# A two-layer streaming-encoder trunk: SSM powers without their zero halves on GpSimd, ScalarE spreading them out, modulation products and norms moved to other places

## The chip, the cores and the metric

One core of a Trainium2 chip runs the whole program in one launch. The time is device microseconds (us), the median of several executions. TensorE (PE) multiplies, VectorE (DVE) and ScalarE (ACT) work elementwise, GpSimd (POOL) too, SyncE (SP) issues DMAs; all five run their own instruction streams and wait for each other by semaphores.

## The reference

`x` is 256 tokens by 1024 channels, float32, batch 1. A conditioning vector `c` gives, for each of the two layers, six rows of 1024 values (shifts, scales, gates) by a 1024 x 6144 product.

```
for layer i:
    mod = silu(c) @ mod_w[i] + mod_b[i];  sh1, sc1, g1, sh2, sc2, g2 = split(mod, 6)
    h = rms_norm(x, g) * (1 + sc1) + sh1
    y = sparse_attention(h)            # layer 0: indexer scores, 64 kept keys per query, ALiBi, softmax
    y = s5_layer(h)                    # layer 1: diagonal complex state space model, gelu, GLU
    x = x + g1 * y
    h = rms_norm(x, g) * (1 + sc2) + sh2
    x = x + g2 * conv_ffn(h)           # up 1024 -> 5632, causal conv of width 3, silu gate, down 2816 -> 1024
return rms_norm(x, final_g)
```

The S5 layer has 64 groups of 16 channels with 64 complex states each: `h[t] = a * h[t-1] + Bbar u[t]`, `y[t] = Re(C h[t]) + d u[t]`. It is computed in chunks of 4 steps, for which the powers `a^k Bbar` and `C a^k`, k = 0 to 4, are needed.

## The kernel before, in words

All weights stream through one ring of six buffers `raw` (128 x 1024 floats, 512 KB each), loaded by SP in the order of use. Each weight tile is split into a rounded high part `whi` by ScalarE (`split_hi`, L749) and a low part `wlo` by VectorE (`split_lo`, L1039), three slots each. TensorE multiplies every tile three times, high by high, high by low and low by high (`three`, L345 to L347), 24 matmuls for one tile of 8 k-blocks. `slot_used`, `hi_ready`, `lo_ready` count tiles. The order on each engine is written out by hand.

The modulation product is cut into 24 pieces `c` (2 MB each), `gemv(c)` (L381): 16 matmuls of 2 columns into the PSUM bank `gv`. After each second piece ScalarE copies `gv` to `gm` (`row_out`), TensorE turns it into columns (`columns`, L392, with a 2-column matrix `picks`), and VectorE adds the bias (`col_out`, L1044). Pieces 0 to 5 stand in the projection phase, 6 to 13 in attention, and 14 to 23 (`C_FFN` = 14) in the first FFN, two for every four steps of its loop.

Phases in order of time: the first norm; six projection tiles in halves (`half(n, 0)`, then pieces 2 and 3 and `columns(1)`, then `half(n, 1)`); the indexer scores with pieces 4 and 5; 24 more projection tiles with the top-k rounds of VectorE; attention over 8 head pairs; the output projection (8 tiles); `norm(1)`; the FFN of layer 0 (22 steps of two up tiles and one down tile each, `up_step` and `down_step`); `norm(2)`; the S5 input projection interleaved with the state space work; the GLU (16 tiles); `norm(3)`; the FFN of layer 1, the same loop with no modulation pieces; the last norm. A norm takes squares on ScalarE (L768), sums them on TensorE into `gv` (L426), makes a column of them (L433), takes the root, and spreads it (L443); then VectorE and ScalarE make `hh` and `hl` for the next product, block by block (`norm_out`, L1063 and L1068; `norm_hi`, L785).

GpSimd makes the powers while the first FFN runs: `times` is one complex product, six instructions of 128 x 1024 (L1545 to L1555). Two groups of 16 channels stand side by side on partitions 0 to 63 and 64 to 127, and in the layout `p (pair, 32 channels)` the half that belongs to the other group is zero; these zeros are loaded and multiplied. There are 43 such instructions before `pw` = `PW_K`; `pace` lets two go for each step of the FFN (it waits on `a_lo`). The last power, six more, comes after `k_done` in `norm(2)`. TensorE uses the powers in `lag_kernels` (L632), which waits for `pw`.

## Time and profile before

| | us |
|---|---|
| median of 3 executions | 802.56 (801.44 to 803.48) |
| the profiled execution | 801.77 |
| its span, first to last instruction | 800.0 |
| PE busy | 742.9 (93%) |
| DVE busy | 584.6 (73%) |
| ACT busy | 389.0 (49%) |
| POOL busy | 175.4 (22%) |

The profile is of one execution. "Busy" excludes waits; the granted clock is a share of TensorE's full speed. A share over the whole span is an average over phases with different limits, so the phases are read one by one.

### The profile page before, as it was taken

Reading aid. Unit: us, or ns where it says so; the run is one execution under the profiler, and the core shown is the slowest. Engines: PE = TensorE matmul, PEld = TensorE weight load, DVE = VectorE, ACT = ScalarE, POOL = GpSimd, SP = SyncE. Lnnn points to the kernel's source line nnn. Section 1 sums busy time; section 2 is a strip of 40 time slices with the busy share of each in tenths; the row PEclk is TensorE's granted clock in tenths of the full one; section 3 lists DMA queues with packets and bytes.
Section 4 is the critical chain, followed back from the end, with each engine's and each line's share of the span. In section 5 each row is a group of like instructions: output and inputs, shape, how many; then the busy total and the mean of one; then the engine's idle time right before and its main releaser. Section 6 shows DMA issues by size and latency. Waiting matters only on the chain.

```text
span 800.0 us, 17708 instructions
## 1 busy us (share of the span) xinstructions
PE 742.9 (93%) x6676; PEld 675.5 (84%) x6676; DVE 584.6 (73%) x948; ACT 389.0 (49%) x656; POOL 175.4 (22%) x115
## 2 busy tenths in 40 slices
PE   5778999999899999999999798989989999999996
PEld 1667999559798889898989688988979999999994
DVE  5666555984778888888998875686657667666675
ACT  4255445555464445444445442324456555555554
POOL 0000000301336444544444515542000000000000
PEclk9889999999899999999999889999999999999998
DMA  9898554896346776767775211112634555555531
GB/s 330 340 350 343 194 182 135 327 401 251 127 168 241 258 258 247 270 242 255 246 259 171 93 53 55 54 56 78 195 124 146 196 174 193 174 178 194 168 100 53
DMA packets 46842, 157.51 MB, mean 197 GB/s; under 512 B 6352, under 2 KB 7888, under 8 KB 46800
## 3 DMA queue, kind: packets, MB, share of 16 engines
q1 hardware_dynamic: 44064, 148.46, 53.3%
q10 hardware_dynamic: 2160, 6.38, 2.0%
q0 software_dynamic: 576, 2.10, 0.7%
q8 instruction: 28, 0.46, 0.2%
q14 instruction: 14, 0.11, 0.0%
HBM read 155.87 MB, written 1.05 MB: 196 GB/s over the span
## 4 chain that ended last, share of the span: by engine, by line
PE 62%; DVE 18%; issue 9%; ACT 6%; DMA 2%; SPq 1%; POOL 1%; DVEq 1%; ACTq 0%; POOLq 0%
PE up L345 10%; PE up L347 10%; PE up L346 10%; DVE wlo L1039 8%; PE acc L345 7%; PE acc L346 6%; PE acc L347 6%; ACT whi L749 3%; DVE ffn L1341 3%; PE gv L381 3%; DVE hl L1068 1%; DMA ffn<-in_mw 1%; DMA arena<-in_mw 1%; PE up L697 1%; PE acc L672 1%
## 5 line engine op out<-in xcount | busy, mean ns | idle before, releaser
L1039 DVE TENSOR_TENSOR wlo<-raw,whi 128x1024 fp32r<-128x1024 f32 x188 | 297.2, 1597 | 93.9 <-ACT whi L749 86.6
L345 PE MATMUL up<-hh,whi 128*128 128x256 f32 x896 | 257.3, 287 | 1.3 <-DVE hl L1068 0.8
L346 PE MATMUL up<-hl,whi 128*128 128x256 f32 x896 | 255.3, 285 | 0.0
L347 PE MATMUL up<-hh,wlo 128*128 128x256 f32 x896 | 255.2, 285 | 0.0
L749 ACT ACTIVATE whi<-raw 128x1024 fp32r<-128x1024 f32 x185 | 191.7, 1051 | 35.7 <-PE acc L347 24.4
L345 PEld LDWEIGHTS up<-hh,whi 128*128 128x128 f32 x896 | 173.8, 194 | 11.5 <-issue 9.9
L346 PEld LDWEIGHTS up<-hl,whi 128*128 128x128 f32 x896 | 173.9, 194 | 0.0
L347 PEld LDWEIGHTS up<-hh,wlo 128*128 128x128 f32 x896 | 173.7, 194 | 0.0
L345 PE MATMUL acc<-ah,whi 128*128 128x256 f32 x352 | 100.4, 285 | 6.8 <-DVE wlo L1039 6.6
L346 PE MATMUL acc<-al,whi 128*128 128x256 f32 x352 | 99.6, 283 | 0.0
L347 PE MATMUL acc<-ah,wlo 128*128 128x256 f32 x352 | 99.5, 283 | 0.0
L1341 DVE SCALAR_TENSOR_TENSOR ffn<-up,conv,ffn 128x254 f32<-128x254 f32 (+1 forms) x176 | 72.5, 472 | 32.3 <-ACT ffn L914 32.3
L345 PE MATMUL acc<-hh,whi 128*128 128x256 f32 x256 | 77.5, 303 | 9.6 <-DVE hl L1068 6.0
L914 ACT ACTIVATE ffn<-up,conv 128x256 f32<-128x256 f32 x88 | 44.9, 560 | 67.4 <-PE up L347 67.3
L346 PE MATMUL acc<-hl,whi 128*128 128x256 f32 x256 | 74.9, 292 | 0.0
L347 PE MATMUL acc<-hh,wlo 128*128 128x256 f32 x256 | 74.7, 292 | 0.0
L345 PEld LDWEIGHTS acc<-ah,whi 128*128 128x128 f32 x352 | 67.5, 192 | 8.4 <-DVE wlo L1039 8.4
L346 PEld LDWEIGHTS acc<-al,whi 128*128 128x128 f32 x352 | 67.5, 192 | 0.0
L347 PEld LDWEIGHTS acc<-ah,wlo 128*128 128x128 f32 x352 | 67.5, 192 | 0.0
L345 PEld LDWEIGHTS acc<-hh,whi 128*128 128x128 f32 x256 | 51.4, 201 | 13.8 <-issue 7.4
L346 PEld LDWEIGHTS acc<-hl,whi 128*128 128x128 f32 x256 | 51.7, 202 | 0.0
L347 PEld LDWEIGHTS acc<-hh,wlo 128*128 128x128 f32 x256 | 51.6, 202 | 0.0
(215 smaller groups left out, 963.1 us busy)
## 6 DMA issues: line engine op xcount, KB each, us to landing
raw<-in_w SPq DMA_DIRECT2D x188, 512.0 KB, 3.4
mraw<-in_mw SPq DMA_DIRECT2D x60, 512.0 KB, 6.2
arena<-in_mw SPq DMA_DIRECT2D x12, 512.0 KB, 11.6
raw<-in_w SPq DMA_DIRECT2D x12, 256.0 KB, 11.4
tmp<-in_mw SPq DMA_DIRECT2D x6, 512.0 KB, 7.7
ffn<-in_mw SPq DMA_DIRECT2D x6, 512.0 KB, 8.6
tmp<-in_mw ACTq DMA_DIRECT2D x4, 512.0 KB, 7.1
ffn<-in_mw ACTq DMA_DIRECT2D x4, 512.0 KB, 9.1
```

Of the source, the lines that this page charges most:

```text
L345: pe.matmul(out, w_h, xh, start=first, stop=False, skip_group_check=skip)
L346: pe.matmul(out, w_h, xl, start=False, stop=False, skip_group_check=skip)
L347: return pe.matmul(out, w_l, xh, start=False, stop=last, skip_group_check=skip)
L381: mm = pe.matmul(gv[32 * j:32 * j + 2, :], cond[:, k, 1 - odd:3 - odd], src[:, kk * 512:kk * 512 + 512], start=(k < 4 and not odd), stop=( ...
L672: mm = pe.matmul(acc[:, 2 + mt % 2, (2 * q + r) * NJ:(2 * q + r + 1) * NJ], bpow_r[:, r, c:c + P], ust[:, mt % 2, q, :], start=True, stop= ...
L697: mm = pe.matmul(y[32 * q:32 * q + 32, :, l], cpow[:, (l + 1) % 4, r, pair * 32:pair * 32 + 32], hst[:, r, q, :], start=False, stop=(l == ...
L749: act.activation(whi[:, n % SPL, :], raw[:, n % RAW, :], ACT.Copy).then_inc(hi_ready, 1)
L914: act.activation(cb[:, par, e, :], up[:, par, e * T:(e + 1) * T], ACT.Identity, scale=conv[:, layer, 2, ds(s + e * FT, 1)], bias=conv[:, l ...
L1039: dve.tensor_tensor(wlo[:, n % SPL, :], raw[:, n % RAW, :], whi[:, n % SPL, :].bitcast(F32), ALU.subtract).then_inc(lo_ready, 1)
L1068: dve.scalar_tensor_tensor(hl[:, k, :], tmp[:, k, :], modc[:, sh + k:sh + k + 1], hh[:, k, :].bitcast(F32), ALU.add, ALU.subtract).then_in ...
L1341: dve.scalar_tensor_tensor(cb[:, par, e, 1 + back:T], up[:, par, e * T:e * T + T - 1 - back], w, cb[:, par, e, 1 + back:T], ALU.mult, ALU. ...
```

## The change

- **Powers.** `b_re`, `b_im`, `c_re`, `c_im` are stored without the zero halves (256 KB each). `times` works on 128 x 512 in `turn_x`, `turn_b`, `turn_c`. After each finished power ScalarE writes it into the old layout: `pad`, two ACTIVATEs with a per-partition factor of 1 or 0 (`sides`), one for each half. In the first FFN a pad stands at the end of steps 5, 8, 11, 14, 15, 18 and 21, an eighth after `split_hi(W_SIN)` and before the squares of `norm(2)`, the ninth in the S5 loop. TensorE waits for `padded`.
- **Modulation pieces.** Piece 14 is multiplied inside `norm(1)` before the last square's sum, 15 after the spread, 16 to 20 in the first FFN, 21 in `norm(2)`, 22 and 23 in `norm(3)`. Pieces 15, 22 and 23 have their own places in `arena`; SP loads 22 and 23 after the S5 loop (`y_done`), ahead of the GLU tiles from the eighth on.
- **Columns.** From pair 2 on, `columns` is four 128 x 128 transposes, and VectorE sums the four partial rows (a reduce and an add in place of one add).
- **Norms.** The sums go to `misc`; the bank openings of the FFN stand in the waits of the norm.
- **First phases.** SP no longer loads the six small constants, GpSimd's queue does; `gemv(2)`, `gemv(3)` and `columns(1)` stand between the first halves; the indexer's scores and `gemv(5)` stand between projection tiles 6 to 11.

```diff
-C_PROJ, C_ATT, C_FFN = 4, 6, 14
+C_PROJ, C_ATT, C_OUT, C_FFN, C_SIN, C_GLU = 4, 6, 14, 16, 21, 22
-        t1, t2 = tpool[:, 0:1024], tpool[:, 1024:2048]
+        t1, t2 = tpool[:, 0:512], tpool[:, 512:1024]
+        turn_x = tpool[:, 1024:2048].rearrange(c_form, r=2, n=PR)
+        turn_b = cpow[:, 3, 0, :].rearrange(c_form, r=2, n=PR)
+        turn_c = cpow[:, 3, 1, :].rearrange(c_form, r=2, n=PR)
...
@@ SP
-            for dst, name in ((ones[:], "ones"), (epsc[:], "epsc"), (picks[:], "picks"), (ident[:], "ident")):
-                sp_.dma_start(dst, t[name]).then_inc(ones_in, 16)
             load_m(0)
-            for dst, name in ((modb[:], "modb"), (gains[:], "gains")):
-                sp_.dma_start(dst, t[name]).then_inc(early_in, 16)
...
+            for n in range(W_SIN, W_GLU + RAW + 1):
                 load_w(n)
-            first = W_SIN + 3
+            sp_.wait_ge(y_done, KT)
+            for c in range(2):
+                for s in range(MS):
+                    sp_.dma_start(last[:, MS * c + s, :], t["mw"][(C_GLU + c) * MS + s, :, :]).then_inc(m_late[1 + c], 16)
+            first = W_GLU + RAW + 1
@@ PE
-                    mm = pe.matmul(misc[:, 2 * q:2 * q + 2], gm[:, q * P:(q + 1) * P], picks[:], start=True, stop=True)
+                    if pair < 2:
+                        mm = pe.matmul(misc[:, 2 * q:2 * q + 2], gm[:, q * P:(q + 1) * P], picks[:], start=True, stop=True)
+                    else:
+                        mm = pe.transpose(misc[:, q * P:(q + 1) * P], gm[:, q * P:(q + 1) * P], ident[:])
...
                 for k in range(KT):
+                    if filler and k == KT - 1:
+                        filler()
                     pe.wait_ge(sq_ready, KT * n + k + 1)
...
-            for n in range(RAW):
-                half(n, 0)
+            half(0, 0)
             pe.wait_ge(gm_ready, 1)
             gemv(2)
+            half(1, 0)
+            half(2, 0)
             gemv(3)
+            half(3, 0)
             pe.wait_ge(hp_ready, 4)
             columns(1)
+            half(4, 0)
+            half(5, 0)
...
+            stream(6)
...
+            score(0, 1, T)
+            stream(7)
+            pe.wait_ge(idx_relu, 1)
+            score(1, 0, P)
+            stream(8)
+            gemv(C_PROJ + 1)
+            stream(9)
+            stream(10)
+            columns(C_PROJ // 2)
+            stream(11)
...
-            norm(1, C_FFN // 2, misc[:, T:2 * T])
+            norm(1, C_OUT // 2, misc[:, T:2 * T], open_rest, open_first, lambda: gemv(C_OUT))
+            gemv(C_OUT + 1)
...
-            for bank in (acc[:, 0, :], acc[:, 1, :], acc[:, 2, :], acc[:, 3, :], up[:, 0, :]):
-                open_bank(bank)
...
-                    with pe.Fori(0, 5) as i:
+                    two_steps(0, (C_OUT // 2, 0))
+                    with pe.Fori(0, 2) as i:
                         gemv(C_FFN, i)
-                        two_steps(2 * i)
+                        two_steps(4 * i + 1)
+                        two_steps(4 * i + 2)
                         gemv(C_FFN + 1, i)
-                        two_steps(2 * i + 1, i)
+                        two_steps(4 * i + 3, (C_FFN // 2, i))
+                        two_steps(4 * i + 4)
+                    gemv(C_SIN - 1)
+                    two_steps(9)
...
-            pe.wait_ge(pw, PW_K)
+            pe.wait_ge(padded, 2 * N_POW)
             lag_kernels(range(0, 5))
-            norm(2, CH, misc[:, T:2 * T], lambda: lag_kernels(range(5, KT - 1)))
+            norm(2, C_SIN // 2, misc[:, T:2 * T], lambda: lag_kernels(range(5, KT - 1)))
+            gemv(C_SIN)
...
                         project_two((acc[:, 0, 0:T], acc[:, 1, 0:T]), W_SIN, 3)
+                        columns(C_SIN // 2)
+                        pe.wait_ge(mod_col, C_GLU // 2)
...
-            norm(3, CH, misc[:, T:2 * T])
+            norm(3, C_GLU // 2, misc[:, T:2 * T], open_rest, open_first, lambda: gemv(C_GLU))
+            gemv(C_GLU + 1)
@@ ACT
+            def pad(src, dst, need):
+                act.wait_ge(pw, need)
+                for g in range(2):
+                    act.activation(dst.rearrange("p r n (g c) -> p r n g c", g=2)[:, :, :, g, :], src, ACT.Identity,
+                                   scale=sides[:, g:g + 1]).then_inc(padded, 1)
+            pads = {5: (turn_x, b_at(0), 6), 8: (turn_b, b_at(1), 12), 11: (turn_x, b_at(2), 18),
+                    14: (turn_b, b_at(3), 24), 15: (turn_c, c_at(0), 25), 18: (turn_x, c_at(1), 31),
+                    21: (turn_c, c_at(2), 37)}
...
+                    if layer == 0 and s in pads:
+                        pad(*pads[s])
...
             split_hi(W_SIN)
+            act.wait_ge(padded, 2 * (N_POW - 1))
+            pad(turn_x, c_at(3), PW_K)
             fetch_root()
...
+                    if m == 1:
+                        pad(raised, c_at(0), PW_ALL)
@@ DVE
+                if pair >= 2:
+                    parts = misc[:].rearrange("p (q j r) -> p r q j", q=4, j=4)[:, 0:2, :, :]
+                    dve.tensor_reduce(gsum[:].rearrange("p (e q) -> p e q", e=2), parts, AX.X, ALU.add).then_inc(part_sum, 1)
+                    dve.wait_ge(part_sum, pair + i - 1)
+                    dve.tensor_tensor(modc[:, ds(8 * (pair + i), 8)], gsum[:], modb[:, ds(8 * (pair + i), 8)],
+                                      ALU.add).then_inc(mod_col, 1)
+                    return
@@ POOL
+            for dst, name in ((ones[:], "ones"), (epsc[:], "epsc"), (picks[:], "picks"), (ident[:], "ident")):
+                pool.dma_start(dst, t[name]).then_inc(ones_in, 16)
...
-                return pr(name).unsqueeze(2).broadcast_to([P, PR, 32])
+                return pr(name).unsqueeze(2).broadcast_to([P, PR, 16])
...
-            pool.wait_ge(mod_used, 2 * CH * MS)
+            pool.wait_ge(mod_used, C_GLU * MS)
             pool.memset(mraw[:].rearrange("p a b -> p (a b)"), 0.0).then_inc(kz, 1)
...
-PW_FREE, PW_STEP = 3, 2
+PW_FREE, PW_STEP = 0, 2
```

## Rows read from the trace of the kernel before

**Rows 1.** Busy time of each engine by stretch; last columns PE clock, DMA share, GB/s

```profile
24.00:68.00 44.00, 36.38 (x255) 28.02 (x256) 27.47 (x58) 15.23 (x27) 0.00 (x0) 0.85 0.93 352
209.00:216.00 7.00, 4.16 (x23) 1.95 (x18) 3.60 (x10) 3.00 (x7) 0.00 (x0) 0.89 0.26 91
216.00:442.00 226.00, 218.69 (x1781) 200.41 (x1781) 197.99 (x218) 111.61 (x168) 104.60 (x41) 0.99 0.66 233
442.00:467.00 25.00, 18.20 (x205) 15.52 (x205) 20.07 (x28) 9.12 (x21) 12.80 (x7) 0.73 0.20 62
597.00:788.00 191.00, 191.00 (x1581) 191.00 (x1582) 133.89 (x213) 107.41 (x163) 0.00 (x0) 0.99 0.48 160
```

**Rows 2.** VectorE's costliest group in the first FFN, then in the second

```profile
L1039 DVE TENSOR_TENSOR wlo<-raw,whi 128x1024 fp32r<-128x1024 f32 x65 | 142.1, 2208 | 14.1 <-ACT whi L749 14.0
...
L1039 DVE TENSOR_TENSOR wlo<-raw,whi 128x1024 fp32r<-128x1024 f32 x64 | 76.6, 1220 | 13.1 <-ACT whi L749 13.0
```

**Rows 3.** VectorE in order of time: start, us, in one step of the first FFN

```profile
297.21 5.96 DVE L1039 TENSOR_TENSOR wlo<-raw,whi 128x1024 fp32r<-128x1024 f32 x2 [0.52 <-ACT whi L749]
303.10 1.64 DVE L1341 SCALAR_TENSOR_TENSOR ffn<-up,conv,ffn 128x255 f32<-128x255 f32 x4
307.72 5.96 DVE L1039 TENSOR_TENSOR wlo<-raw,whi 128x1024 fp32r<-128x1024 f32 x2 [0.52 <-ACT whi L749]
```

**Rows 4.** GpSimd in order of time: two of the 1024-wide products, one 512-wide

```profile
296.83 2.41 POOL L1555 TENSOR_TENSOR arena<-arena 128x1024 f32<-128x1024 f32 x1 [5.25 <-DVE al L1350]
299.32 2.78 POOL L1545 TENSOR_TENSOR arena<-arena,prm 128x1024 f32<-128x1024 f32 x1
485.97 1.28 POOL L1586 TENSOR_TENSOR arena<-tmp,arena 128x512 f32<-128x512 f32 x1 [2.02 <-DVE tmp L1439]
```

**Rows 5.** TensorE in order of time: a modulation piece and a `columns` of the first FFN

```profile
229.77 1.90 PE L381 MATMUL gv<-mraw,cond 128*2 128x512 f32 x16
427.12 0.95 PE L392 MATMUL misc<-picks,gm 128*128 128x2 f32 x8
```

**Rows 6.** ScalarE in order of time, in a step of the second FFN and after the first

```profile
707.15 1.99 ACT L749 ACTIVATE whi<-raw 128x1024 fp32r<-128x1024 f32 x2
711.01 1.02 ACT L914 ACTIVATE ffn<-up,conv 128x256 f32<-128x256 f32 x2 [1.86 <-PE up L347]
...
438.50 1.04 ACT L749 ACTIVATE whi<-raw 128x1024 fp32r<-128x1024 f32 x1
439.56 1.28 ACT L780 ACT_TABLE_LOAD   x1
441.23 3.16 ACT L768 ACTIVATE tmp<-x 128x256 f32<-128x256 f32 x8 [0.17 <-DVE x L1321]
```

**Rows 7.** TensorE in order of time, first phases

```profile
40.34 1.02 PE L392 MATMUL misc<-picks,gm 128*128 128x2 f32 x8 [0.79 <-issue]
44.67 0.55 PE L454 MATMUL acc<-hh,whi 128*128 128x256 f32 x1 [3.31 <-DVE hl L1180]
58.80 0.41 PE L481 MATMUL misc<-ident,arena 128*128 128x128 f32 x2 [0.62 <-ACT arena L839]
63.33 1.03 PE L381 MATMUL gv<-ffn,cond 128*2 128x512 f32 x4 [1.18 <-DMA ffn<-in_mw]
68.35 0.36 PE L345 MATMUL up<-hh,whi 128*128 128x256 f32 x1
```

**Rows 8.** Stretches of 1 us: PE busy first, granted clock third from the end

```profile
46.00:47.00 1.00, 1.00 (x6) 1.00 (x6) 1.00 (x3) 0.24 (x1) 0.00 (x0) 0.50 1.01 406
51.00:52.00 1.00, 1.00 (x11) 1.00 (x10) 0.41 (x1) 0.67 (x2) 0.00 (x0) 1.00 1.01 324
```

**Rows 9.** TensorE in order of time, `norm(1)`

```profile
210.58 0.59 PE L426 MATMUL gv<-tmp,ones 128*1 128x256 f32 x2 [1.32 <-ACT tmp L768]
213.77 1.27 PE L397 MATMUL acc<-zrow 1*128 1x512 bf16 x4
215.63 0.55 PE L345 MATMUL up<-hh,whi 128*128 128x256 f32 x1 [0.17 <-DVE hl L1068]
```

**Rows 10.** TensorE in order of time, after `norm(2)`

```profile
451.97 0.36 PE L345 MATMUL acc<-hh,whi 128*128 128x256 f32 x1 [2.48 <-DVE hl L1068]
```

More of the change, by code:

```diff
@@ L209, in build @@
         m_loaded = [sem(f"m_loaded{j}") for j in range(MS)]
+        m_late = [sem(f"m_late{j}") for j in range(3)]
         m_odd = [sem(f"m_odd{j}") for j in range(MS)]
@@ L477, in _, with score @@
                     gemv(C_PROJ)
-            pe.wait_ge(mod_col, C_PROJ // 2)
-            pe.wait_ge(qkv_ready, RAW)
-            for qt in range(2):
-                mm = pe.transpose(misc[:, qt * P:(qt + 1) * P], qkv[:, S_WI, qt * P:(qt + 1) * P], ident[:])
-            mm.then_inc(idx_done, 1)
-            for step, (qt, keys) in enumerate(((1, T), (0, P))):
-                if step:
-                    gemv(C_PROJ + 1)
-                    pe.wait_ge(idx_relu, 1)
+            def score(step, qt, keys):
                 for h in range(IH):
@@ L1221, in _ @@
                         dve.scalar_tensor_tensor(out, r, wit[:, qt, h:h + 1], out, ALU.mult, ALU.add).then_inc(idx_acc, 1)
-            col_out(C_PROJ // 2)
+                split_lo(10 + step)
             dve.wait_ge(idx_acc, 16)
@@ L1227, in _, with last_round, top_round @@
             dve.wait_ge(sel, 2)
+            def last_round(i, n):
+                dve.wait_ge(sel, 2 + 8 * (i - 1) + 2 * n)
+            def top_round(n):
+                for qt, off, keys in ((0, 0, T), (1, T, P)):
+                    sc = scr[:, off:off + keys]
+                    if n % 2 == 0:
+                        dve.max(max8[:, qt, :], sc).then_inc(sel, 1)
+                    else:
+                        dve.match_replace(sc, max8[:, qt, :], sc, TAKEN).then_inc(sel, 1)
+            split_lo(12)
+            last_round(1, 0)
+            top_round(0)
+            split_lo(13)
+            last_round(1, 1)
+            top_round(1)
+            col_out(C_PROJ // 2)
+            last_round(1, 2)
+            top_round(2)
+            split_lo(14)
+            last_round(1, 3)
+            top_round(3)
             def top_k(i, slots):
@@ L1563, in _ @@
             pool.wait_ge(prm_v, PRM_STEPS)
             pool.wait_ge(ssm_in, 16 * N_SSM)
-            times(b_at(0), c_at(1), "cre", "cim", False)
-            for k in range(3):
-                times(b_at(k + 1), b_at(k), "are", "aim", False)
+            times(turn_x, turn_b, "cre", "cim", False)
+            times(turn_b, turn_x, "are", "aim", False)
+            times(turn_x, turn_b, "are", "aim", False, free=1)
+            times(turn_b, turn_x, "are", "aim", False, free=2)
             pace()
-            step(pool.tensor_scalar(cpow[:, 0, 1, :], cpow[:, 0, 1, :], -1.0, None, ALU.mult))
@@ L1570, in _ @@
-            for k in range(3):
-                times(c_at(k + 1), c_at(k), "are", "aim", True)
+            step(pool.tensor_scalar(turn_c[:, 1], turn_c[:, 1], -1.0, None, ALU.mult))
+            times(turn_x, turn_c, "are", "aim", True, free=3)
+            times(turn_c, turn_x, "are", "aim", True, free=5)
+            times(turn_x, turn_c, "are", "aim", True, free=6)
             assert cnt[0] == PW_K
-            pool.wait_ge(mod_used, 2 * CH * MS)
+            pool.wait_ge(mod_used, C_GLU * MS)
```

223 lines of the change are left out of this document (142 added, 81 removed).

## The prediction

> **What bounds the kernel now.** I read three things, in this order: busy time by stretch, then VectorE's groups in the two FFNs, then TensorE, ScalarE and GpSimd in order of time at the seams. TensorE is busy 93% of the span, so the question is in which stretches it works on something that can go, or stands. The two FFNs make the comparison: both do 66 weight tiles, the second takes 191 us with TensorE never idle, the first 226 us with 7.3 us idle [rows 1]. The difference of 35 us is what this change is mostly about. The first one carries ten modulation pieces and five `columns`; a piece is 1.83 us where pieces follow each other (1.90 with its tail) and a `columns` 0.95 [rows 5], which makes 18.3 + 4.8 = 23.1 us. The other 12 us come from VectorE: there the low parts `wlo` cost 2208 ns each against 1220 ns in the second FFN [rows 2], 65 x 0.99 = 64 us more, in the only FFN in which GpSimd works (104.6 us busy). A step of VectorE lasts 307.72 - 297.21 = 10.5 us, in which two `wlo` take 5.96 us [rows 3] while GpSimd's two instructions take about 2.4 + 2.8 us [rows 4]. Without GpSimd the two take 2.4 us (2 x 1220 less their overlap), so one step of VectorE is 10.5 - 3.6 = 6.9 us. TensorE's own step is 191 / 22 = 8.7 us, and with the pieces 8.7 + 23.1 / 22 = 9.7 us. So the first FFN is paced now by VectorE, by 0.3 to 0.8 us a step, and TensorE is close behind.
>
> Elsewhere TensorE is idle in the first 68 us (44 - 36.4 = 7.6 us of the second stretch, at a mean clock of 0.85, with the DMA engines 93% busy), in 209 to 216 (2.8 us) and in 442 to 467 (6.8 us at a mean clock of 0.73) [rows 1].
>
> **The change part by part.** The sum is made against the profiled execution, 801.77 us (span 800.0 and 1.77 around it), which lies 0.79 us under the median of 802.56, a tenth of a per cent.
>
> *First FFN.* Five of its ten pieces stay (16 to 20): 5 x 1.83 = 9.2 us go. Three `columns` in place of five, about 1.9 us go; that they are transposes now is worth at most a few tenths of 0.95 us either way. GpSimd's instructions have half the elements. What one costs the trace brackets: half of 1.92 to 2.41 us, 1.0 to 1.2, if it goes by elements, and 1.28 us by the row of a 512-wide product [rows 4]. Of GpSimd's 5.2 us a step 3.6 came back as `wlo` time, a share of 0.7. With 2.2 to 2.6 us a step VectorE gets 1.5 to 1.9 us more, a step of 6.9 + 1.5 to 1.9 = 8.4 to 8.8 us, beside TensorE's 8.7 + (9.2 + 2.9) / 22 = 9.2 us. TensorE becomes the bound, narrowly. The new work on ScalarE, two `pad` ACTIVATEs of 1024 elements, is not in the trace; the nearest row is the copy `whi` of the same size, 1.05 us, two for 1.99 [rows 6]. Lower bound is that, 2.1 us a pad; upper bound twice it, since the output is written in runs of 16 elements. In a step ScalarE waits 1.86 us for TensorE after the two `whi` copies [rows 6], and that is exactly where the pad stands, so seven pads cost 0.2 us each at the lower end and 2.3 us each at the upper, part of which three slots of `whi` and `wlo` take up. I take 2.1 us, and allow 2.5 us in all for pads and for steps without a piece, in which VectorE's 8.8 is the slower. The FFN becomes 191 + 9.2 + 2.9 + 2.5 = 205.6 us, 20.4 less; ends: 223 (VectorE or ScalarE still paces, 3 less) and 203 (23 less). I take 19 less, because GpSimd's row of 1.28 us is an instruction really seen.
>
> The Trainium skill's page "SBUF — State Buffer", section "SBUF: two separate sides", gives the reason for the two prices of `wlo`: VectorE instructions with two SBUF inputs and GpSimd instructions that read SBUF take a shared port pair as a whole, and one waits for the other. The 5.96 against 2.4 us agree with it [rows 3]. The same section warns of DMAs issued from GpSimd, whose descriptors wait while VectorE holds that pair; that speaks against moving the six constants there. By it they might come one or two instructions of VectorE late, at most 2 us at the start; no row here shows it.
>
> *First phases.* SP issues `x` and then six small DMAs around piece 0; without them the big loads start about 2 us sooner, worth 1 us in a stretch that the DMA engines fill. TensorE stands 3.31 us before the second halves [rows 7] and then works at half the clock until 51, 0.50 against 1.00 [rows 8], 6 us that cost 3. In the new order `columns(1)` is done while halves 4 and 5 remain, 2.9 us at full clock, which cover the 3.3 us of VectorE's and ScalarE's chain, so both should go. Between 58.2 and 68.35 TensorE has 6.2 us of work and stands 4.0 us [rows 7], for copies, for the relu and for a DMA of piece 5; projection tiles of 2.88 us each stand in all these waits now. That makes 1 + 3.3 + 3 + 4 = 11.3. Against it: `gemv(2)` comes before its data is there, up to 2 us. And the stretch is 93% DMA [rows 1]: it moved 23.7 MB by 68 us; at the 406 GB/s of the fullest rows [rows 8] that is 58 us and 3 us of start, so if all of it had to be there the gain is no more than 68.35 - 61 = 7. A part is prefetch. I take 10 less; ends 4 and 13.
>
> *Attention.* Four `col_out` and the fifth before it get a reduce and a wait, about 0.3 us each on an engine that is nearly full there, less 0.1 us each on TensorE: 0.7 more; ends 0 and 2.
>
> *norm(1).* TensorE waits 1.32 us for the last square [rows 9]; piece 14 (1.83) stands there: 0.5 more. The openings, 1.9 us at 213.77, go into waits, and piece 15 takes their place in front of the first product at 215.63 [rows 9]: nothing. Because TensorE stands less, its clock may stay up, worth up to 3.4 us here; I count none of it. Together 0.5 more.
>
> *norm(2).* Here the change costs something that its list doesn't show. After the last `ah`, ScalarE now has the pad of step 21, `split_hi(W_SIN)`, the eighth pad, the table load, and only then the squares, which start at 441.23 now [rows 6]: two pads of 2.1 are 4.2 us late, all on the path, since the root waits for the squares. Back comes: GpSimd's powers, 12.8 us busy in this stretch, slowed each `hl` of VectorE; now it first clears `mraw`, after piece 21, and its six shorter products start some 4 us later, behind most of the `hl`. The eight blocks then take about 0.8 to 1.0 us each instead of the 15.1 us from 451.97 to 467 [rows 10 and 1] if the clock stays up, 12 us if it falls. Piece 21 lies in the wait of 2.48 us. Then `columns` and `mod_col`, 1.7 us of waiting. So 4.2 + 1.7 - 3 to 6.5: between 0.5 less and 3 more; I take 1.5 more.
>
> *GLU and norm(3).* Pieces 22 and 23, 4.2 MB, go ahead of the eighth GLU tile at 547; at 400 GB/s 10.5 us, and the tile is wanted some 16 us after: up to 2 us of stall, I take 1. Piece 22 before the last square costs 1.83 less the 0.6 us wait, 1.2 more; the third `columns` group is now in the second FFN, 0.9 more.
>
> Sum: -19 - 10 + 0.7 + 0.5 + 1.5 + 1 + 1.2 + 0.9 = -23.2. 801.77 - 23.2 = 778.6; from the median 779.4. Since I counted no clock gain in `norm(1)` and `norm(3)`, up to 5 us together, I set 2 of it: **777 us**.
>
> **The rivals.**
>
> *A: the seams give all.* The clock stays up through the three norms and the second halves, VectorE is well under TensorE in the first FFN: -23 - 12.5 - 5 + 4 = -36, 766 us. For it: TensorE's gaps in the new norms are below 1 us each. Against: the two late pads, and TensorE idle at 442 while it waits for the eighth.
>
> *B: the first FFN stays paced by VectorE and ScalarE, the start by DMA.* If a short GpSimd product costs 1.4 us or more beside VectorE, or a pad 3 us, then a step takes 9.7 instead of 9.2: 11 us of the 19 stay away, and 3 of the 10 at the start. -23.2 + 14 = -9: 793 us at worst, 788 in its middle. For it: 1.28 us for 512 elements is two thirds of the cost of 1024, not half [rows 4]. Against: a share of 0.7 came back, not all of it.
>
> *C: the pads become the bound, and the whole is slower.* The place is ScalarE's row of a step, the price each us that a pad takes over 2.1: seven in the loop and two on the path of `norm(2)`, 9 us for each us. To undo 23 us a pad must take 2.1 + 23 / 9 = 4.7 us; at 6 us the time is 802 + 12 = 814. For it: writes in short runs on ScalarE are not in the trace. Against: the same engine writes `cb` and `kbd` at the copy's rate.
>
> *D: the shorter products are not shorter* (their cost is fixed by the instruction): the FFN saves only what the pieces give, 226 - 11 = 215, the sum is -14 and the time 788. The rows of 512 and 1024 elements speak against it; it has 3 of the 23 in 100 that I give B.
>
> **How the numbers follow.** The forecast (770 to 783) has 0.53, A 0.18, B with D 0.23, C 0.04; 0.02 is left for gains and losses that meet near zero. Own range of the forecast 770 to 784; for 8 in 10 I reach half way into A and B: 763 to 790. A measurement here tells 0.3%, 2.4 us, from no change. Faster 0.94, same 0.02, slower 0.04.
>
> **What would show it.** `wlo` in the first FFN at 1.5 to 1.7 us mean instead of 2.2; GpSimd's product at 1.0 to 1.3 us; the FFN at 203 to 209 us with TensorE idle under 3; the pad at 1.05 us per ACTIVATE; the squares of `norm(2)` starting 4 us later after the last `ah`; no wait of 3 us before the second halves, and the first tile of the full stream reached, its inserted work included, 10 us sooner; no half clock there. The prediction is wrong if steps of the first FFN are still above 9.6 us with VectorE waiting for nothing, if a pad takes over 3 us, if the GLU's eighth tile waits more than 3 us for its DMA, or if the constants hold up the first sums past 9 us.

## The result, and the profile after

| | before | after |
|---|---|---|
| median of the runs side by side | 803.02 us (801.44 to 803.57) | 771.47 us (770.57 to 773.63) |
| ratio, 95% interval | | 0.9614 (0.9589 to 0.9639) |
| profiled execution, its span | 801.77, 800.0 us | 771.09, 769.3 us |

The forecast was 777.0 us, its range 763 to 790. The kernel got 30.7 us shorter in the span, not 23 to 25. TensorE's matmuls cut the span into seven stretches, and one table serves for this and for the first experiments (us, from the times of TensorE's first or last instruction of each stretch; each column is one execution):

| stretch | before | after | powers alone | all but powers | pads twice |
|---|---|---|---|---|---|
| start to first attention scores | 138.3 | 132.6 | 139.0 | 134.1 | 134.2 |
| to the first FFN, `norm(1)` in it | 77.3 | 77.8 | 76.2 | 77.1 | 77.2 |
| first FFN | 226.9 | 203.9 | 216.4 | 224.7 | 211.3 |
| to the transposes, `norm(2)` in it | 24.5 | 20.0 | 20.5 | 18.1 | 24.4 |
| state space and GLU | 123.1 | 124.3 | 121.1 | 124.4 | 124.9 |
| `norm(3)` | 6.6 | 7.3 | 7.2 | 7.3 | 7.3 |
| second FFN to the end | 203.2 | 203.5 | 203.5 | 203.3 | 203.5 |

The same windows as in [rows 1], of the kernel after: the first phases, `norm(1)`, the first FFN, what follows it, the second FFN.

```profile
24.00:68.00 44.00, 39.92 (x299) 31.19 (x300) 30.50 (x62) 18.93 (x32) 0.98 (x2) 0.92 0.93 350
203.00:211.00 8.00, 7.84 (x68) 3.08 (x67) 3.24 (x10) 3.23 (x7) 0.00 (x0) 1.00 0.59 215
211.00:414.00 203.00, 201.82 (x1673) 192.92 (x1672) 158.44 (x215) 123.15 (x177) 67.00 (x43) 1.00 0.65 225
414.00:436.00 22.00, 18.05 (x255) 13.48 (x257) 15.92 (x35) 14.13 (x28) 9.70 (x7) 1.00 0.23 73
566.00:757.00 191.00, 190.05 (x1581) 189.79 (x1581) 133.86 (x214) 107.55 (x163) 0.00 (x0) 1.00 0.49 160
```

TensorE stands 1.2 us of the 203 in the first FFN, where it stood 7.3 of 226, and its granted clock is 1.00 at the two seams where it was 0.89 and 0.73. The groups that answer to [rows 2] (VectorE in the first FFN), and one step after [rows 3] and [rows 4] (VectorE, GpSimd, ScalarE in order of time):

```profile
L1141 DVE TENSOR_TENSOR wlo<-raw,whi 128x1024 fp32r<-128x1024 f32 x64 | 100.3, 1584 | 17.3 <-ACT whi L813 17.3
```

```profile
292.20 4.01 DVE L1141 TENSOR_TENSOR wlo<-raw,whi 128x1024 fp32r<-128x1024 f32 x2 [0.52 <-ACT whi L813]
...
291.82 1.06 POOL L1693 TENSOR_TENSOR arena<-arena,prm 128x512 f32<-128x512 f32 x1 [7.36 <-DVE al L1484]
292.96 2.16 POOL L1695 TENSOR_TENSOR arena<-arena 128x512 f32<-128x512 f32 x1
...
293.70 2.17 ACT L988 ACTIVATE arena<-arena,sides 128x1024 f32<-128x1024 f32 x2
```

Two low parts take 4.01 us where they took 5.96, while GpSimd's two instructions last 3.2 us; a pad is 2.17 us. Where the change lost time, TensorE in the first phases and in the GLU:

```profile
9.79 2.16 PE L465 MATMUL misc<-tmp,ones 128*1 128x256 f32 x16 [9.79 <-DMA ident<-in_ident]
...
24.46 0.35 PE L493 MATMUL acc<-hh,whi 128*128 128x256 f32 x1 [2.29 <-DVE hl L1287]
...
25.82 0.58 PE L493 MATMUL acc<-hh,whi 128*128 128x256 f32 x1 [0.77 <-DVE hl L1287]
...
27.28 0.58 PE L493 MATMUL acc<-hh,whi 128*128 128x256 f32 x1 [0.45 <-DVE hl L1287]
...
532.43 0.36 PE L364 MATMUL acc<-hh,whi 128*128 128x256 f32 x1 [2.85 <-DVE wlo L1141]
```

The blocks of the first half projections come 1.45 us apart. Behind the first FFN, ScalarE and TensorE in order of time:

```profile
413.26 2.17 ACT L988 ACTIVATE arena<-arena,sides 128x1024 f32<-128x1024 f32 x2
415.45 1.28 ACT L844 ACT_TABLE_LOAD   x1
...
416.85 2.54 ACT L832 ACTIVATE tmp<-x 128x256 f32<-128x256 f32 x8
...
426.13 0.38 PE L364 MATMUL acc<-hh,whi 128*128 128x256 f32 x1
```

The squares start 2.5 us after TensorE's last matmul of the FFN (414.30), where they started 1.3 us before it (441.23 [rows 6] against 442.57): 3.9 us later, as forecast. Still the stretch is shorter.

Single executions differ. In seven kernels whose state-space part and GLU order are alike, the stretch "state space and GLU" took 122.8 to 126.1 us, and in seven whose first phases are alike the first scores started at 132.1 to 134.2 us. A difference of 1 or 2 us between two columns is therefore read only where a wait or an instruction in the rows shows it.

### The profile page after: what moved, and what is told of

The parts are those of the page before. It is cut to its first block, busy times and chain, and to the rows that moved or that the text cites. A ratio compares the mean times of both kernels' runs of the same rounds, so it can differ in the third digit from the quotient of the medians.

```text
span 769.3 us, 17309 instructions
## 1 busy us (share of the span) xinstructions
PE 723.5 (94%) x6636; PEld 656.4 (85%) x6636; DVE 539.0 (70%) x959; ACT 407.4 (53%) x674; POOL 129.8 (17%) x121
## 3 DMA queue, kind: packets, MB, share of 16 engines
q0 software_dynamic: 512, 1.25, 0.5%
HBM read 154.82 MB, written 1.05 MB: 203 GB/s over the span
## 4 chain that ended last, share of the span: by engine, by line
PE 80%; DVE 8%; ACT 4%; DMA 4%; issue 2%; SPq 1%; POOL 1%; DVEq 0%; ACTq 0%; POOLq 0%
PE up L364 14%; PE up L366 14%; PE up L365 14%; PE acc L364 8%; PE acc L365 8%; PE acc L366 8%; PE gv L406 4%; DMA raw<-in_w 1%; DMA ffn<-in_mw 1%; DVE tmp L1172 1%; DVE hl L1177 1%; DVE wlo L1141 1%; ACT whi L813 1%; PE acc L733 1%; DMA ident<-in_ident 1%
## 5 line engine op out<-in xcount | busy, mean ns | idle before, releaser
L1141 DVE TENSOR_TENSOR wlo<-raw,whi 128x1024 fp32r<-128x1024 f32 x188 | 252.2, 1356 | 99.1 <-ACT whi L813 94.3
L364 PEld LDWEIGHTS up<-hh,whi 128*128 128x128 f32 x896 | 171.8, 192 | 10.1 <-issue 4.1
L365 PEld LDWEIGHTS up<-hl,whi 128*128 128x128 f32 x896 | 171.9, 192 | 0.0
L364 PE MATMUL acc<-hh,whi 128*128 128x256 f32 x256 | 74.6, 291 | 6.7 <-DVE hl L1589 3.6
L365 PE MATMUL acc<-hl,whi 128*128 128x256 f32 x256 | 72.4, 283 | 0.0
L366 PE MATMUL acc<-hh,wlo 128*128 128x256 f32 x256 | 72.3, 283 | 0.0
L364 PEld LDWEIGHTS acc<-hh,whi 128*128 128x128 f32 x256 | 48.9, 191 | 10.3 <-issue 7.9
L365 PEld LDWEIGHTS acc<-hl,whi 128*128 128x128 f32 x256 | 49.0, 191 | 0.0
L366 PEld LDWEIGHTS acc<-hh,wlo 128*128 128x128 f32 x256 | 49.0, 191 | 0.0
```

The costliest lines, as they stand in the source:

```text
L364: pe.matmul(out, w_h, xh, start=first, stop=False, skip_group_check=skip)
L365: pe.matmul(out, w_h, xl, start=False, stop=False, skip_group_check=skip)
L366: return pe.matmul(out, w_l, xh, start=False, stop=last, skip_group_check=skip)
L1141: dve.tensor_tensor(wlo[:, n % SPL, :], raw[:, n % RAW, :], whi[:, n % SPL, :].bitcast(F32), ALU.subtract).then_inc(lo_ready, 1)
```

## The experiments

Ratios are to the kernel before in the same sitting. "After" in a sum is its 771.47 us.

**1. Powers alone.** The kernel before with half-size products and pads, the rest untouched.

```
-        t1, t2 = tpool[:, 0:1024], tpool[:, 1024:2048]
+        t1, t2 = tpool[:, 0:512], tpool[:, 512:1024]
...
+                    if layer == 0 and s in pads:
+                        pad(*pads[s])
```

> The kernel before with one part of the change alone: GpSimd makes the state-space powers without their zero halves, ScalarE spreads them out. My theory: the first FFN got 23 us shorter from two things together, shorter low halves on VectorE (their mean fell from 2208 to 1584 ns) and fewer modulation pieces for TensorE and VectorE. With the first alone, the mean of the low halves falls to 1.55 to 1.7 us and VectorE is no longer what a step waits for, but TensorE still carries all its pieces there, so the first FFN falls only from 227 to 214 to 218 us; after it the pads cost 1 to 4 us. Sum: 8 us under the kernel before, 795 us (791 to 798). Rival 1, the low halves were the whole of it: the first FFN falls to about 206 us, and the kernel runs at 783 us. Rival 2, the low halves got shorter through something else in the change: their mean stays above 2.0 us, and the time stays within 2 us of the kernel before, or above it by the pads (803 to 806 us).

787.08 us, ratio 0.9821 (0.9789 to 0.9853). That is outside the 791 to 798 us expected, and nearer to rival 1's 783; the length of the first FFN, 216.4 us, is what decides between the two.

**2. All but powers.** The changed kernel with full-width products, without pads.

```
-                return pr(name).unsqueeze(2).broadcast_to([P, PR, 16])
+                return pr(name).unsqueeze(2).broadcast_to([P, PR, 32])
...
-                    if layer == 0 and s in pads:
-                        pad(*pads[s])
```

> The changed kernel with the powers made as before (1024 elements wide, zeros and all, no pads), everything else kept. My theory: the mean of the low halves in the first FFN goes back to about 2.2 us and VectorE sets the step again, but with fewer pieces than before: 0.6 us more per low half times 64 is 38 us of VectorE work, of which VectorE had some 15 to 25 us free. The first FFN takes 214 to 220 us instead of 204; after it the pads' 4 us come back. Sum: 8 us over the changed kernel, 779 us (775 to 785). Rival, the pieces and the early loads alone had made the first FFN short: it stays within 2 us of 204 us, and without the pads the kernel is at 767 us, faster than the changed one.

791.78 us, ratio 0.9886 (0.9848 to 0.9923). The first FFN of the kernel before, of powers alone, of all but powers and of the kernel after, each in the columns of [rows 1] (TensorE, its loads, VectorE, ScalarE, GpSimd busy):

```profile
215.63:442.57 226.94, 219.63 (x1788) 201.22 (x1792) 198.93 (x220) 112.27 (x170) 104.60 (x41) 0.99 0.66 232
```

```profile
215.18:431.53 216.35, 216.35 (x1784) 199.69 (x1784) 154.82 (x215) 125.09 (x179) 70.13 (x44) 0.99 0.68 243
```

```profile
211.19:435.89 224.70, 207.14 (x1684) 194.53 (x1684) 201.74 (x222) 110.77 (x169) 108.66 (x43) 1.00 0.60 205
```

```profile
210.42:414.30 203.88, 202.69 (x1680) 193.59 (x1676) 159.32 (x216) 123.75 (x177) 67.00 (x43) 1.00 0.65 225
```

With the powers alone TensorE is busy all of the 216.4 us: it is the bound and it still carries its ten pieces. Without them TensorE has 12.5 us less to do (219.6 against 207.1), but VectorE is busy for 202 us, and 17.6 us of TensorE's stretch go to waiting. Alone the parts took 10.6 and 2.2 us off this stretch, together 23.1. That is the theory's claim. Rival 1 of run 1 wanted an FFN of about 206 us, rival 2 a mean over 2.0 us for the low parts; both fell. My size for run 2 was wrong: I gave 214 to 220 us. VectorE does not use a step fully even where it is the bound (202 of 225 us busy); I had counted such time as free.

Over the whole first FFN the low parts' means are 2208 ns (before) and 2144 (all but powers) with full-width products, 1524 (powers alone) and 1578 (after; the row of it shown above ends at 411 us and has 1584) with half-width ones: the width decides, and what else was changed moves them by 3%. The rows of powers alone and of all but powers:

```profile
L1068 DVE TENSOR_TENSOR wlo<-raw,whi 128x1024 fp32r<-128x1024 f32 x65 | 98.7, 1524 | 29.2 <-ACT whi L755 29.0
```

```profile
L1135 DVE TENSOR_TENSOR wlo<-raw,whi 128x1024 fp32r<-128x1024 f32 x65 | 137.9, 2144 | 11.6 <-ACT whi L813 11.6
```

Run 1 was 8 us faster than I expected, and that came from outside the FFN: 4.0 us behind it, where I had put a loss of 1 to 4, and 2.0 in the state-space part and the GLU, which the powers' half size or the spread between executions may account for: not shown which. In run 2 the pads' absence brought 1.9 us behind the FFN.

**3. Pads twice.** Two more ACTIVATEs of the same size in front of each pad.

```
+                if need < PW_ALL:
+                    for g in range(2):
+                        act.activation(tmp8[:, 0:1024].rearrange("p (r n c) -> p r n c", r=2, n=PR), src, ACT.Identity,
+                                       scale=sides[:, g:g + 1]).then_inc(again, 1)
```

> The changed kernel with each pad up to the eighth preceded by two more ACTIVATEs of the same size into a scratch tile (2.2 to 2.3 us more of ScalarE each). My theory: in the first FFN ScalarE had 1.76 us of slack ahead of chain_a, which hides most of a second pad, so the seven pads there cost 0 to 0.7 us each (0 to 5 us); after the first FFN the eighth pad lies on the path with its whole length, 1 to 2.3 us. Sum 2 to 6 us over the changed kernel, 775 us. Rival 1, ScalarE already sets the step wherever a pad falls: 8 x 2.25 = 18 us more, 789 us. Rival 2, the pads are hidden everywhere (the state-space part waits for something else): 771 to 772 us.

783.98 us, ratio 0.9773 (0.9746 to 0.98): 12.5 us more, beyond my 2 to 6. The first FFN got 7.4 us longer for seven doses of 2.3 us, so nearly half of each reaches the end. Behind the FFN 4.4 us: the dose fell there twice, since the seventh pad too comes after the last chain. TensorE's first instruction there, in this kernel and then in the one after:

```profile
428.28 1.10 PE L692 MATMUL up<-arena 128*32 128x128 f32 x16 [5.56 <-ACT arena L996]
```

```profile
415.48 2.46 PE L692 MATMUL up<-arena 128*32 128x128 f32 x80 [1.19 <-ACT arena L988]
```

ScalarE's slack in a step (1.76 us before `chain_a`) is shorter than one pad (2.17 us), and of a second one nearly half is paid. Rival 1's full price holds only at the seam (the few microseconds between two phases).

**4. Tiny products.** One instruction of six; the other five alike. The kernel leaves out 31 of 32 pairs of the powers, so only its time means something.

```
-                step(pool.tensor_tensor(w3(t1), src[:, 0], wide(re), ALU.mult))
+                step(pool.tensor_tensor(w3(t1)[:, 0:1], src[:, 0, 0:1], wide(re)[:, 0:1], ALU.mult))
```

> The changed kernel in which each of GpSimd's product instructions of the powers covers one pair of 32 only, so that GpSimd is nearly idle in the first FFN; 31 of 32 pairs of the powers are left out. My theory: TensorE now sets the step of the first FFN (it has almost no gap there), so the low halves get shorter still, to about 1.3 us on the mean, and the first FFN gets at most 2 us shorter: 769 to 771 us. Rival, VectorE's sharing with GpSimd still paces the first FFN as it did before, only less: it falls by 0.3 us x 64 = 19 us at most, to 190 to 197 us, and the kernel to 758 to 764 us.

770.48 us, ratio 0.9607 (0.9573 to 0.964), not to be told from the kernel after. The first FFN:

```profile
210.85:413.99 203.14, 202.19 (x1680) 193.50 (x1676) 135.50 (x216) 123.78 (x178) 11.53 (x43) 1.00 0.66 226
```

VectorE has 24 us less to do than in the kernel after, and it buys 0.7 us. The low parts fall to a mean of 1224 ns:

```profile
L1141 DVE TENSOR_TENSOR wlo<-raw,whi 128x1024 fp32r<-128x1024 f32 x65 | 79.0, 1224 | 24.6 <-ACT whi L813 24.4
```

In the second FFN of the kernel before it is 1220 [rows 2]. The change has taken all but 0.7 us of what there is to take from GpSimd's work in this loop.

**5. Constants on SP.**

```
+            for dst, name in ((ones[:], "ones"), (epsc[:], "epsc"), (picks[:], "picks"), (ident[:], "ident")):
+                sp_.dma_start(dst, t[name]).then_inc(ones_in, 16)
```

> The changed kernel with the six constants issued by SP again, where they stood before the change. My theory: at the start they cost more on GpSimd's queue than on SP's, since norm 0's first sum waits for ident at 9.79 us where it started at 7.64 us before. The first sum comes 1.5 to 2.1 us sooner, and the kernel is 1.5 us faster, 770.0 against 771.5 us. Rival, it was x that arrived late (ScalarE's squares start at 8.33 us instead of 6.83) because all 16 transfers meet whatever the queue: then the first sum moves by less than 0.5 us and the time stays.

770.57 us (769.13 to 774.77), ratio 0.9621 (0.9594 to 0.9648): no difference that these runs can tell. TensorE at the start of this kernel:

```profile
7.79 2.49 PE L469 MATMUL misc<-tmp,ones 128*1 128x256 f32 x16 [7.79 <-DMA ident<-in_ident]
...
18.01 1.03 PE L410 MATMUL gv<-arena,cond 128*2 128x512 f32 x4 [0.16 <-DMA arena<-in_mw]
19.29 1.03 PE L410 MATMUL gv<-arena,cond 128*2 128x512 f32 x4 [0.25 <-DMA arena<-in_mw]
21.08 1.05 PE L422 MATMUL misc<-picks,gm 128*128 128x2 f32 x8 [0.76 <-ACT gm L823]
```

The first sum comes 2.0 us sooner, as expected, and at 21.08 us nothing of it is left: `columns(0)` started at 21.12 in the kernel after. Piece 1 now waits for its own transfers, and they are the bound of this stretch: it ends at 20.3 us in both kernels. Of the rival the result was right and the reason half right. The first sum did move, but `x` was late too: ScalarE's squares start at 6.67 us here and at 8.33 in the kernel after, 0.72 us of it a wait for `x`. Which of the two holds the first sum changes from execution to execution: with the constants on GpSimd's queue it starts at 9.40 to 10.73 us in nine kernels, in five of them at the squares and not at `ident`; with SP's queue at 7.49 to 8.03 in four.

**6. One block ahead.**

```
-                first_low(4 * h)
-                for k in range(4 * h + 1, 4 * h + 4):
-                    first_scaled(k)
+                first_scaled(4 * h + 1)
+                for k in range(4 * h, 4 * h + 4):
                     first_low(k)
+                    if k + 2 < 4 * h + 4:
+                        first_scaled(k + 2)
```

> The changed kernel with VectorE's scaled block k+1 put ahead of its low block k in the first two half projections (as one step of a pipeline ahead). My theory: the change made the blocks a serial chain over VectorE, ScalarE and VectorE, 1.45 us each where they came every 0.87 us; undone, the eight blocks of the first halves come 0.4 to 0.6 us sooner each, and first attention scores start 2 to 3.5 us sooner: 768.5 us. Rival, TensorE has modulation pieces to fill the gaps, and ends the first phase by its own work: less than 0.7 us.

767.24 us (765.49 to 769.8), ratio 0.9571 (0.9547 to 0.9595). Scores start at 128.83 instead of 132.61 us, 3.8 us sooner, although the first sum came 0.7 us later in this execution. VectorE's blocks in this kernel, then in the kernel after:

```profile
24.73 0.48 DVE L1287 SCALAR_TENSOR_TENSOR hl<-tmp,modc,hh 128x256 fp32r<-128x256 f32 x1
...
25.52 0.48 DVE L1287 SCALAR_TENSOR_TENSOR hl<-tmp,modc,hh 128x256 fp32r<-128x256 f32 x1
```

```profile
23.83 0.49 DVE L1287 SCALAR_TENSOR_TENSOR hl<-tmp,modc,hh 128x256 fp32r<-128x256 f32 x1
...
25.29 0.48 DVE L1287 SCALAR_TENSOR_TENSOR hl<-tmp,modc,hh 128x256 fp32r<-128x256 f32 x1 [0.57 <-ACT hh L880]
```

0.79 against 1.46 us a block (24.73 to 25.52, 23.83 to 25.29). The ratio's interval just touches that of the kernel after (0.9589 to 0.9639), but the 3.8 us stand clear of the 132.1 to 134.2 us at which scores start without this edit, and runs 9 and 10 have them too (128.4 and 128.9).

**7. GLU order.**

```
-            for n in range(W_SIN, W_GLU + RAW + 1):
+            for n in range(W_SIN, W_GLU + RAW + 3):
```

> The changed kernel with two more weight tiles of the GLU loaded ahead of SP's wait for the end of the state-space outputs and the sixteen modulation tiles behind it. My theory: the 2.85 us for which TensorE waits at 532.43 us is SP's order (ScalarE waits 7.56 us there for raw from in_w), and it goes whole: 768.6 us. Rival, the tiles are late because the transfers are: the modulation tiles then come later into norm 3, whose pieces wait, and the sum stays within 0.7 us.

768.93 us (767.83 to 770.61), ratio 0.9594 (0.9572 to 0.9615). The GLU's last fourteen tiles, here and in the kernel after:

```profile
515.13:555.89 40.76, 40.76 (x340) 40.46 (x344) 24.46 (x29) 22.49 (x32) 0.00 (x0) 1.00 0.77 278
```

```profile
514.75:558.58 43.83, 40.98 (x340) 40.52 (x344) 24.19 (x29) 22.39 (x32) 0.00 (x0) 1.00 0.78 283
```

The wait is gone: TensorE is busy for all of its 40.8 us, 3.1 us less than in the kernel after. No piece in `norm(3)` waits for its load either. Two things keep this from being 3.1 us of the kernel's time. The wait itself is 1.2 to 3.1 us in the traces of the kernels that leave this order alone (1.18 in run 6, 1.41 in run 5, 1.73 in run 8, 2.85 in the kernel after, 3.05 in run 11). And in this execution `norm(3)` took 8.85 us instead of 7.25, at a mean granted clock of 0.81 instead of 1.00, of which the second FFN gave 1.3 back:

```profile
555.89:564.74 8.85, 8.68 (x63) 2.62 (x62) 4.41 (x13) 4.07 (x10) 0.00 (x0) 0.81 0.20 62
```

The ratios, 0.9594 (0.9572 to 0.9615) and 0.9614 (0.9589 to 0.9639), overlap: that the wait is gone is shown by the trace, what it is worth in the whole is not told by these runs.

**8. Pads sooner.**

```
-            pads = {5: (turn_x, b_at(0), 6), ...
+            pads = {2: (turn_x, b_at(0), 6), ..., 20: (turn_x, c_at(3), 43)}
...
-            act.wait_ge(padded, 2 * (N_POW - 1))
-            pad(turn_x, c_at(3), PW_K)
...
-PW_FREE, PW_STEP = 0, 2
+PW_FREE, PW_STEP = 6, 2
```

> The changed kernel with GpSimd's first products begun in the attention part and every pad three steps sooner, so that the eighth pad lies inside the first FFN and none between its end and norm 2. My theory: with no pads at all the stretch from the end of the first FFN to the transposes took 18.1 us instead of 20.0, so the two pads there cost 1.9 us, of which the first accounts for most: 1 to 2 us faster, 770 us. It would be more if products in the attention part were free of charge, less if GpSimd's products there slow down VectorE's chains: rival, VectorE's work in the attention part is on the path, each of the early products costs it up to 0.8 us, and the kernel gets 0 to 3 us slower.

767.13 us (766.65 to 770.58), ratio 0.9579 (0.9555 to 0.9603). From the FFN's end to the transposes 16.9 us instead of 20.0; the attention part is not longer (77.1 against 77.8), so the rival fell; the ratio's interval overlaps that of the kernel after (0.9589 to 0.9639), and the gain rests on the seam in the trace. ScalarE and TensorE at the seam:

```profile
411.30 1.28 ACT L844 ACT_TABLE_LOAD   x1
...
412.97 3.16 ACT L832 ACTIVATE tmp<-x 128x256 f32<-128x256 f32 x8 [0.17 <-DVE x L1453]
...
414.04 2.46 PE L692 MATMUL up<-arena 128*32 128x128 f32 x80
```

The squares stand before the FFN's last matmul again (414.11), and TensorE goes on without a gap. The two pads at the seam had cost 3.1 of their 4.3 us. The other 1.1 us of the 4.3 is the GLU's wait (1.73 us here, not 2.85), which this edit does not touch and which is within its spread from run to run. I had expected 1 to 2 us by the comparison with run 2, in which full-width products lay in the same stretch.

**9, 10. Three and four of these together.** The edits of runs 6 to 8, then those of run 5 as well.

```
+                    if k + 2 < 4 * h + 4:
+                        first_scaled(k + 2)
...
+            for n in range(W_SIN, W_GLU + RAW + 3):
...
+PW_FREE, PW_STEP = 6, 2
```

> The changed kernel with three of the mends together: the scaled blocks one ahead, two more GLU tiles ahead of the wait, the pads and products sooner; the constants stay on GpSimd's queue. My theory: the three lie in stretches apart (first phase, GLU, norm 2) and each gave 2.5 to 4.3 us under 771.5 alone (4.2, 2.5 and 4.3; part of the last is the GLU's wait, which was 1.1 us shorter there), so together 9 to 10.5 us: 761.5 us. Rival, what a mend wins is given back where TensorE's clock or the loads come next: 765 to 768 us.

761.38 us (761.22 to 761.91), ratio 0.9496 (0.9478 to 0.9515).

> The same three mends and the six constants back on SP's queue. My theory: alone the constants' move to SP brought the first sum 2.0 us sooner, and the stretch to columns(0) gave all of it back (21.08 against 21.12 us), with 769.1 to 774.8 us in all; with the blocks one ahead it is the same: within 0.7 us of the kernel with three mends. Rival, the 2 us at the start are worth their length as soon as the low blocks are no longer a chain: 1.5 to 2 us faster than with three, near 759.5 us.

760.72 us (760.17 to 762.96), ratio 0.9491 (0.947 to 0.9512). Runs 6 to 8 lay 4.2, 2.5 and 4.3 us under the kernel after, 11.1 together, and three at once give 10.1. But these medians are of other sittings, in which the kernel before was 1.0 to 1.4 us faster than beside the kernel after. By the ratios the single mends are worth 3.5, 1.6 and 2.8 us, 7.9 together, and three at once 9.5; with intervals of some 2 us to either side that is no more than a sum. With the chain of blocks gone the constants' queue still makes no difference. Three mends is the version to keep: 5% under the kernel before and 1.2% under the changed one (0.9496 over 0.9614, with intervals that lie apart).

**11. Plain norms.**

```
-            norm(1, C_OUT // 2, misc[:, T:2 * T], open_rest, open_first, lambda: gemv(C_OUT))
+            norm(1, C_OUT // 2, misc[:, T:2 * T])
+            gemv(C_OUT)
             gemv(C_OUT + 1)
+            open_first()
+            open_rest()
```

> The changed kernel with the first modulation piece and the bank openings taken out of norm 1 and norm 3 and put behind them. My theory: norm 1 then idles as before (1.3, 0.5 and 0.9 us), with one piece (1.9 us) and the openings (1.9 us) behind it on the path, in both norms: 3 to 4 us each less what they hid, that is +5 to +7 us, and if a stretch at half clock follows, as it did in some of the norms before, up to 3 us more: 777.5 us (775 to 781). Rival, the pieces filled time in which TensorE would have waited for VectorE's first hl block anyway: +2 us or less.

775.78 us (772.14 to 777.15), ratio 0.967 (0.9646 to 0.9693): 4.3 us more. `norm(1)` and `norm(3)` in this kernel, then in the kernel after:

```profile
203.55:212.49 8.94, 7.53 (x61) 2.48 (x62) 5.52 (x15) 4.67 (x10) 0.00 (x0) 1.00 0.27 97
561.03:572.12 11.09, 9.16 (x61) 2.93 (x62) 7.04 (x17) 5.31 (x12) 0.00 (x0) 0.85 0.15 48
```

```profile
203.17:210.42 7.25, 7.09 (x62) 2.43 (x62) 2.66 (x8) 2.93 (x6) 0.00 (x0) 1.00 0.58 205
558.58:565.83 7.25, 7.09 (x62) 2.42 (x62) 3.06 (x9) 3.27 (x8) 0.00 (x0) 1.00 0.22 72
```

1.7 and 3.8 us more. The FFNs behind them give back 1.4 and 1.5 us, of which 0.96 and 0.95 are the wait of TensorE behind the first tile in the kernel after, which is not here. That leaves 2.6 us that these traces place at the two norms; by the medians the whole is 4.3 us slower. The rest of the profiled pair's difference lies in stretches whose code is the same (1.2 us before the first scores, 1.8 in the state space and GLU, 0.8 less in attention), so what the fillers (the piece and the openings that fill the norm's waits) are worth is 2.6 to 4.3 us. The rival (+2 or less) falls by the medians, and my 5 to 7 was too much. The two norms differ in idle time and in clock: 1.4 us idle at 1.00 cost 1.7 us, 1.9 us idle and a mean of 0.85 cost 3.8, so some 1.6 us of `norm(3)`'s is clock (0.5 us being the longer idle time). They do not hold the clock up for certain: of ten profiled kernels with the fillers in `norm(3)`, six took 7.25 us at 1.00 and four took 8.2 to 8.9 at 0.81 to 0.88.

## Why the prediction was right, and where not

*First FFN: taken -19, own estimate 205.6 us; measured -23.1, 203.9 us.* Right in the mechanism. VectorE paced it before and TensorE paces it now; the low parts' mean of 1578 ns lies in the forecast's 1.5 to 1.7; two low parts lengthened by 1.6 us a step, forecast 1.5 to 1.9; five pieces and two `columns` were to be worth 11.1 us, and the kernel with the powers alone is 12.5 us longer there. What I had not said is that either part alone gives little: the gain of 23 is 10.6 + 2.2 and 10 more for both. Two terms were sized too carefully. Of the 2.5 us allowed for pads and for steps without a piece 0.8 were needed (203.9 - 191 - 9.2 - 2.9). And I had drawn back from my own estimate toward GpSimd's row of 1.28 us: beside VectorE its instructions do take that and more (means of 1312 to 1785 ns, over my sign of 1.0 to 1.3 and mostly over rival B's condition of 1.4), but tiny products show that only 0.7 us hung on it. The Trainium skill's page "SBUF — State Buffer", section "SBUF: two separate sides", names the shared port pair as the reason; the means of 2208, 1578 and 1224 ns with full, half and nearly no GpSimd work agree with it.

*`norm(2)`: taken +1.5, ends -0.5 and +3; measured -4.5.* The step that failed is the size of what comes back, "3 to 6.5". The late pads cost what I said: the squares are 3.9 us later, and moving the pads brings 3.1 back. But the projection takes 6.84 us, not 15.1, so 8.2 came back there, and 1.5 more between the squares and the first product, against 1.3 for `columns` and the wait behind it: 3.9 - 8.2 - 1.5 + 1.3 = -4.5. My own blocks of 0.8 to 1.0 us, eight of them in 15.1 us, give 7.1 to 8.7; the sum took 3 to 6.5 without saying why. So the mechanism was there and its size was not carried into the sum. VectorE's `hl` in the kernel before, in powers alone and in the kernel after, with GpSimd in the last:

```profile
452.14 1.74 DVE L1068 SCALAR_TENSOR_TENSOR hl<-tmp,modc,hh 128x256 fp32r<-128x256 f32 x1
```

```profile
443.52 0.89 DVE L1097 SCALAR_TENSOR_TENSOR hl<-tmp,modc,hh 128x256 fp32r<-128x256 f32 x1
```

```profile
426.66 0.48 DVE L1177 SCALAR_TENSOR_TENSOR hl<-tmp,modc,hh 128x256 fp32r<-128x256 f32 x1
...
425.91 3.52 POOL L1717 MEMSET mraw<- 128x4096 f32 x1 [25.92 <-PE gv L406]
```

At 0.79 us a block (0.48 and a scaled block before it, overlapped) VectorE runs ahead of TensorE, which waits 0.3 us in the whole projection, at a granted clock of 1.00; before it stood 3.5 of the 15.1 us, at 0.55. Over the whole stretch the clock is 1.00 after, 0.72 before, 0.92 with the powers alone.

*First phases: taken -10, ends -4 and -13; measured -5.7.* "No wait of 3 us before the second halves" came true, and the clock is 1.00 there. What I overlooked is in the change itself: a block's scaled form is made only after the last one's low form, a chain over VectorE, ScalarE and VectorE of 1.45 us a block. Mended it gives 3.8 us more, 9.5 in all, near the 10 taken; the runs do not split this into my terms of 1, 3.3, 3 and 4. The last of them was misread: between 58.2 and 68.35 us TensorE stands 2.8 us and not 4.0 (7.38 us busy of 10.17). "The big loads start about 2 us sooner" came true (SP issues the first at 2.61 us, not 4.50), and the 1 us that it should bring did not: piece 1 ends at 20.3 us, before the change at 19.6. The constants held the first sum until 9.79 us, past the 9 us that I had named as a sign against me, but it cost nothing, since piece 1's transfers end the stretch either way. That this delay is near the 2 us I had allowed is luck: I had put it down to instructions of VectorE in the way, and VectorE ran nothing from 2.3 to 7.16 us, while GpSimd issued the six constants from 1.25 to 4.10 us. That is why a sign at one instruction is weaker than one at the end of its stretch.

*The rest.* Attention and `norm(1)`: +0.5, taken +1.2. State space and GLU +1.1, taken +1; the GLU's wait is 2.85 us, within the 3 I had named, its cause SP's order as forecast, and the rest of the stretch was 1.7 shorter, which is within what this stretch varies by. `norm(3)` +0.7, taken +1.2. Second FFN +0.3, taken +0.9. Of the clock in the norms I took 2 of 5; plain norms put the fillers at 2.6 to 4.3 us, clock and filled waits together. Rivals B, C and D fell: neither VectorE nor a pad (2.17 us, where C needed 4.7) set the step. (D's sum was added up wrongly: 8 us less of the first FFN's 19 makes -15, not -14.) The time lies half way between the forecast and rival A (766), whose reason was right for the norms and the FFN and wrong for the first phases.

## What to carry to other kernels

When two engines are within a few per cent of each other in a loop, price their reliefs together: here 10.6 and 2.2 us alone became 23.1, and an experiment that undoes one part shows its value only beside the other. Work hung on an engine with slack is cheap once (at most 0.8 us for seven pads in the loop), costs nearly half its length the second time, and most of it where it falls behind the last chain of a loop (3.1 of 4.3 us): put such work a few steps sooner. Before counting microseconds saved at the start, find what ends the stretch: 2.0 us won by a first sum were worth nothing behind a transfer that did not move.
